# Two transformer blocks on one core: the adaLN chunks inside the layers in runs of four instead of runs of two

## The reference

```python
for l in range(2):
    shift, scale, gate = split(silu(c) @ ada_w[l] + ada_b[l], 3)          # adaLN, and the same with c_ctx
    h  = rmsnorm(x, norm_g[l]) * (1 + scale) + shift                      # latent and context rows
    q, k, v, u_pool, u_fourier, g = split(h @ w_in[l])
    mixed = concat(attention(q, k, v), pooling(u_pool), fourier(u_fourier))
    x = x + gate * ((mixed * silu(g)) @ w_out[l])                         # context too, in layer 0
x = rmsnorm(x, final_norm_g)
```

## Time and profile before

| | us |
|---|---|
| median of 3 runs (2392.55 to 2397.18) | 2396.88 |
| the profiled execution | 2403.58 |
| its span | 2401.8 |
| PE busy | 2313.1 (96%) |
| DVE busy | 1307.1 (54%) |
| ACT busy | 1046.8 (44%) |
| POOL busy | 266.3 (11%) |

### The profile page before, as it was taken

The page is one execution under the profiler, slowest core; times in us unless marked ns, Lnnn a source line. Parts: engine busy times, 40 slices in busy tenths (PEclk is TensorE's granted clock), DMA queues, the critical chain, the costliest instruction groups (busy, mean ns, idle before and its releaser), DMA issues.

```text
span 2401.8 us, 30909 instructions
## 1 busy us (share of the span) xinstructions
PE 2313.1 (96%) x12239; PEld 1860.4 (77%) x12239; DVE 1307.1 (54%) x2098; ACT 1046.8 (44%) x1606; POOL 266.3 (11%) x333
## 2 busy tenths in 40 slices
PE   5879999999999999999999998999999999999998
PEld 2457777677777866778888886888888888888887
DVE  2444533142333264544776767667765777567764
ACT  2222333242322155445554465555544555345543
POOL 1000100000001022100010424111100110001111
PEclk8889999999999999999999998999999999999999
DMA  9774443334665465734566544565555565565552
GB/s 367 268 258 163 146 137 129 108 131 150 211 205 171 168 233 177 267 103 141 186 192 215 172 149 149 176 183 186 187 183 186 185 189 184 186 187 184 188 186 87
DMA packets 347023, 436.68 MB, mean 182 GB/s; under 512 B 13848, under 2 KB 269280, under 8 KB 345984
## 3 DMA queue, kind: packets, MB, share of 16 engines
q1 hardware_dynamic: 341376, 413.19, 52.2%
q0 software_dynamic: 3408, 16.38, 1.8%
q10 hardware_dynamic: 2096, 5.15, 0.6%
HBM read 428.37 MB, written 6.29 MB: 181 GB/s over the span
## 4 chain that ended last, share of the span: by engine, by line
PE 87%; DVE 5%; DMA 3%; ACT 3%; issue 1%; POOL 1%; SPq 0%; ACTq 0%; POOLq 0%
PE ps L1280 31%; PE ps L1281 15%; PE ps L1255 5%; PE ps L1256 5%; PE ps L1257 5%; PE ps L1275 5%; PE ps L1277 5%; PE ps L1276 5%; PE ps L1236 3%; DVE SPL L1714 2%; DMA RAW<-in_w_in_dram 2%; ACT SPL L1480 2%; PE ps L1329 1%; PE ps L1346 1%; DMA RAW<-in_ada_w_dram 1%
## 5 line engine op out<-in xcount | busy, mean ns | idle before, releaser
L1280 PE MATMUL ps<-HS,SPL 128*128 128x512 f32 x3456 | 1228.7, 400 | 13.8 <-DVE SPL L1714 9.3
L1714 DVE TENSOR_TENSOR SPL<-RAW,SPL 128x1024 fp32r<-128x1024 f32 x592 | 752.0, 1274 | 635.7 <-ACT SPL L1480 633.3
L1281 PE MATMUL ps<-HS,SPL 128*128 128x256 f32 x3456 | 970.2, 281 | 0.0
L1480 ACT ACTIVATE SPL<-RAW 128x1024 fp32r<-128x1024 f32 x592 | 621.3, 1055 | 476.0 <-PE ps L1281 291.2
L1280 PEld LDWEIGHTS ps<-HS,SPL 128*128 128x128 f32 x3456 | 651.2, 188 | 177.3 <-issue 6.9
L1281 PEld LDWEIGHTS ps<-HS,SPL 128*128 128x128 f32 x3456 | 654.6, 189 | 2.2 <-issue 1.9
L1255 PE MATMUL ps<-SPL,HS 128*128 128x512 f32 x576 | 249.7, 434 | 21.3 <-ACT XT L1522 7.5
L1257 PE MATMUL ps<-SPL,HS 128*128 128x512 f32 x576 | 230.2, 400 | 0.0
L1256 PE MATMUL ps<-SPL,HS 128*128 128x512 f32 x576 | 230.0, 399 | 0.0
L1275 PE MATMUL ps<-HS,SPL 128*128 128x512 f32 x480 | 199.9, 416 | 1.2 <-DVE HS L1870 1.2
L1277 PE MATMUL ps<-HS,SPL 128*128 128x512 f32 x480 | 187.8, 391 | 0.0
(11 more groups left out here) (271 smaller groups left out, 1717.7 us busy)
## 6 DMA issues: line engine op xcount, KB each, us to landing
RAW<-in_w_in_dram SPq DMA_DIRECT2D x208, 512.0 KB, 5.8
RAW<-in_ada_w_dram SPq DMA_DIRECT2D x192, 512.0 KB, 4.8
RAW<-in_ffn_w_up_dram SPq DMA_DIRECT2D x192, 512.0 KB, 3.6
RAW<-in_w_out_dram SPq DMA_DIRECT2D x96, 512.0 KB, 4.3
RAW<-in_ffn_w_down_dram SPq DMA_DIRECT2D x96, 512.0 KB, 3.3
x_spill<-XT POOLq DMA_DIRECT2D x2, 2048.0 KB, 15.0
XT<-x_spill POOLq DMA_DIRECT2D x1, 4096.0 KB, 15.8
MM<-in_x_dram ACTq DMA_DIRECT2D x2, 1024.0 KB, 11.3
```

Source lines behind the costliest of these rows:

```text
L1280: mm(PS[b][:, :], wr, hh, start=k == 0, stop=False, skip_group_check=True)
L1281: m = mm(PS[b][:, 256:512], wl, hh[:, 0:256], start=False, stop=k == KT - 1, skip_group_check=True)
L1480: act(SPL[:, (n - 1) % NSPL, 0, :], raw_of(i), ACT.Copy).then_inc(s_hi, 1)
L1714: tt(w[:, 1, :], raw_of(s["i"]), w[:, 0, :].bitcast(F32), ALU.subtract).then_inc(s_lo, 1)
```

## The change

`mixed` puts adaLN chunks between layer chunks. It counts all chunks that stand in the list so far. Before: as soon as that count, divided by 4, leaves 2, two adaLN chunks follow, which gives two layer chunks, two adaLN chunks, and so on. Now: as soon as the count, divided by 8, leaves 4, four adaLN chunks follow, which gives four layer chunks, four adaLN chunks, and so on. The number of both and the ratio of one to one stay as they are.

```diff
             for c in main:
                 seq.append(c)
-                if len(seq) % 4 == 2:
-                    seq.extend(left[:2])
-                    del left[:2]
+                if len(seq) % 8 == 4:
+                    seq.extend(left[:4])
+                    del left[:4]
             return seq
```

## The result

The changed kernel takes **2447.18 us** (median of 4 runs, 2446.34 to 2451.53), the kernel before 2396.97 beside it: ratio 1.0223, 95% interval 1.0203 to 1.0243. That is slower by 50.2 us. The profiled execution took 2451.53 us, its span is 2449.7 (before: 2403.58 and 2401.8).

What follows compares the result with a forecast made beforehand. PE was taken as the bound, busy throughout layer 0's output projection. Terms -10.9 + 25 + 12.4 + 3.6 + 4.5 + 17 gave +51.6 us on the median 2396.88: 2448 us, range 2418 to 2470.

Steps and rivals of the forecast that it cites:

- Split written behind the group's end: At group ends, the next split queues on ACT behind work that empties PSUM, so PE waits; sized separately for each place.
- Output projection, +25: Layer 0's output projection, 7 group ends: PE waits 3.7 us for the split at six, 3.0 at the first; +25 us.
- Gates, +12.4: Layer 0's 8 gate groups: four waits of 1.55 us, attention 2.8, and 3.4 behind the last group; +12.4 us.
- Projections, +3.6: Layer 0's projections: waits of 1.05 us behind q0 and q1, attention behind four splits 0.5 three times; +3.6 us.
- Layer 1, +4.5: Layer 1's 8 runs: +1.9 behind kv, +1.05 at q0, +1.6 into kv, the others nothing; +4.5 us.
- Joining, -10.9: All adaLN runs: joining two runs of two into one of four saves 0.35 us, 62 runs become 31; -10.9 us.
- Clock, +17: PE's clock halves behind long waits: all seven in the output projection, half of five others, 1.8 us each; +17 us.
- Rival 1: Whole kernel: the waits come but PE's clock holds; 2431 us, chance 0.22.
- Loads, nothing: Loads of eight chunks now come in one burst per period; in layer 1 they need 318 GB/s; counted as nothing.
- Rival 3: Loads cost too: bursts at 250 GB/s lengthen layer 1's periods, 29 us more; 2477 us, chance 0.08.
- rival B: Follow-up runs' rival, no chance given: joining saves nothing, the measured 0.35 us being a difference of place; 2397 within 2.

Runs made afterwards that it cites:

- Experiment 6: The kernel after, with the list of splits looked through six chunks ahead in place of five (7 where it was 6): 2394.35 us, ratio 0.9995.
- experiment 5: The kernel before, runs of two kept, with a reach of three chunks for splits in layer 0's output projection alone: 2442.53 us, ratio 1.0194.
- experiment 4: The kernel after, with POOL's sum of squares in layer 0 on one column in place of 512: 2429.30 us, ratio 1.0148.
- exp. 2: The kernel before, runs of two, with the list of splits looked through nine chunks ahead: 2423.97 us, ratio 1.0113.
- exp. 7: The kernel after, with the list of splits looked through seven chunks ahead in place of five (8 where it was 6): 2396.34 us, ratio 1.0000.
- exp. 8: Runs of four in layer 0 alone with a reach of seven there, layer 1 as in the kernel before: 2393.52 us, ratio 0.9986.
- exp. 10: The kernel before, with runs of one adaLN chunk in place of two: 2467.38 us, ratio 1.0315.
- experiments 1: The kernel after, with the list of splits looked through nine chunks ahead in place of five: 2436.41 us, ratio 1.0162.

## Why the prediction was right

The forecast was 2448, slower, and it came out at 2447.2. The mechanism was right; the agreement within 1 us is partly luck, since terms were off by 2 to 5 us in both directions, and the clock came out right for reasons that were partly wrong. By its steps:

- **Split written behind the group's end.** Right in kind, place and size. Experiment 6 undoes only this and returns to the time before; experiment 5 does only this and loses 45.
- **Output projection, +25.** Measured 25.3: six of 3.70 or 3.71, and 3.09 where 3.0 was taken. That 0.9 of each comes from POOL's sum beside the split was put to the test in experiment 4.
- **Gates, +12.4.** Four waits of 1.61 (forecast 1.55). PE went on at 657.26, 7.85 behind the last gate group's run, forecast 7.9. Attention behind four splits was estimated at 2.8; the trace shows 0.44 + 0.20 = 0.6. The estimate charged DVE's whole row of splits to PE.
- **Projections, +3.6.** Three waits of 1.13 where two of 1.05 were counted. Behind gf the Fourier task was counted as a cover and doesn't stand there. The mid-group estimates (three of 0.5 for attention) were nothing.
- **Layer 1, +4.5.** kv 2.0 (forecast 1.9), into kv 7.1 in place of 5.9 (+1.2, forecast 1.6). Behind q0, where I had 1.05 for a split, PE waits 3.19 for L1490 (0.83 in the kernel before, at 886.61); in the middle of q0, where I had nothing, it waits 1.66 at 915.77 for a split that stands behind tiles of HS (L1498, L1501) on ACT. The step looked at each group's last copy, not at all that shares ACT's queue with the splits.
- **Joining, -10.9.** The rate of 0.35 holds where PE is undisturbed (0.36 in the gates), and the traces show the whole of it once waits and clock are taken out. The table below takes the touched part, from the last matmul that all kernels have in common to the start of the last run in layer 1 (169.2 to 1001.4 us in the kernel before, 166.5 to 1049.5 in the kernel after). The last column is what is left of the difference in length when PE's idle time (length less busy) and the clock loss are taken off; the work is the same in all, but for the number of runs.
- **Clock, +17.** The clock loss is 27.3 - 6.8 = 20 us, but 3.9 of the 27.3 and 1.5 of the 6.8 fall into PE's own waiting, so it is 18 us net. I had seven output waits at 1.8 and half of five others. It fell behind all seven, for 17 us in all from 680 to 875, 2.4 each in place of 1.8, since three stayed low about twice as long; behind the gates' four and kv it fell not once (550.02 took 0.47), where I had put 4.5; and 3.4 more than before came at the last gate group and in layer 1, where I had nothing. The term was right by errors that cancel. Rival 1, that the clock holds, was wrong by these rows.
- **Loads, nothing.** PE waited for DMA 9.0 us as before, all in the start. Rival 3 didn't occur.

| kernel | touched part, us | PE idle | clock loss | length against before | idle and clock against before | left |
|---|---|---|---|---|---|---|
| before | 832.2 | 14.5 | 6.8 | | | |
| runs of two, reach nine (exp. 2) | 861.2 | 36.2 | 13.7 | +29.0 | +28.6 | +0.4 |
| runs of four, reach six (exp. 6) | 833.1 | 21.0 | 10.2 | +0.9 | +9.9 | -9.0 |
| runs of four, reach seven (exp. 7) | 831.1 | 21.6 | 8.5 | -1.1 | +8.8 | -9.9 |
| the same in layer 0 alone (exp. 8) | 828.4 | 16.6 | 8.5 | -3.8 | +3.8 | -7.6 |
| runs of one (exp. 10) | 901.9 | 13.1 | 5.1 | +69.7 | -3.1 | +72.8 |
| after | 883.0 | 58.3 | 27.3 | +50.8 | +64.3 | -13.5 |
| two late splits (exp. 5) | 876.8 | 45.4 | 25.5 | +44.6 | +49.6 | -5.0 |

With no joining next to nothing is left (+0.4); with 31 joinings 9.0 and 9.9 us are saved (forecast 10.9), with 23 of them 7.6 (forecast 8.1), and 62 runs more cost 72.8 (71 by the count). So with a reach of six or seven the joinings are not lost: new waits, at L1490 and in attention, and falls of the clock take 9 to 10 us back. That joining saves nothing, rival B of experiments 1 and 2, is out too. The last two rows, with seven falls behind long waits each, need the part of the clock loss that falls into PE's idle time and is counted twice: 3.9 us in the kernel after and 5.9 in experiment 5, 1.5 in the kernel before. Without it -11.1 is left for the 31 joinings of the kernel after and -0.6 where no run was joined; in the other rows it changes what is left by 0.4 to 1.9 us. The two rows without a joining tell how far the last column can be trusted: about 2 us. (The work behind the touched part, the same in all, took from 1387.5 to 1400.3 us in these executions, so whole spans of single traces can't be compared this finely.)

The sum was right partly because small terms cancelled: 2.2 too much at attention, 2.8 too little in layer 1 (2.0 + 1.2 + 2.4 + 1.7 = 7.3 against 4.5). The main term was right since it was read as a time line of four engines and not as a sum of durations. The rule of the Trainium skill (TensorEngine Tiling (Array Packing), Key Properties), that a change of tiling mode drains the array, goes with the trace: a run of 4 narrow matmuls and one of 8 take nearly the same 0.98 and 1.00 us until the next wide one. The rule says nothing on what decided here, where the splits stand.

## What to carry to other kernels

Before regrouping work on the bounding engine, ask for each helper instruction what it is written behind, and whether something there waits for that engine: in a queue that goes in order, the reach of a look-ahead has to grow with the length of the run. Here one chunk of reach, a number beside the change, decided 50 us. More than needed is harmful too, since an early instruction that waits for a load holds up all behind it (28 us with a reach of nine). And a small saving per transition is to be priced at both ends of the step: from one chunk to two it was worth 75 us, from two to four 9 to 10, which new waits and falls of the clock took back.

## What the runs showed of the hardware

- **A run of narrow matmuls has a least time.** 4 matmul records with 128x32 weights (one adaLN chunk) take 0.98 us until the next wide matmul, 8 take 1.00 (724.95 to 725.95 in the kernel before), 16 take 1.85. From 4 to 8 the added work costs 0.02 us.
- **The clock falls on a narrow edge of waiting.** Behind a run of 16 narrow matmuls, waits of 1.6 us were followed by a fall in 0 of 4 cases, waits of 2.85 or so in 2 of 7 (experiment 4), and of 3.09 to 3.71 in 7 of 7. After a run of 8, waits of 3.9 to 4.6 brought it in 7 of 7. Yet in the kernel before it fell at 651.29 behind a wait of 1.18 that followed other short work, in experiment 6 it fell in a wait of 2.25 for L1490 (883.00), and in experiment 4 a wait of 3.19 for L1490 (915.51) brought no fall. So the length of the last wait alone doesn't decide. What does stays open.
- **A fall can come late and stay longer.** In the kernel after, behind the waits that end at 715.82 and 805.22 the first matmul took 0.47 us, still at the full clock, and the first of 0.63 came 1.5 and 0.8 us later; at other groups the clock was down when PE went on (745.50). The clock loss of a fall is 1.7 us at some groups and 3.4 at others.
